# NSA gates projected inside the first query products, in two PSUM banks, with another order of weight splits around the compression

## The chip, the cores and the metric

The kernel runs on one core of one Trainium2 chip. The metric is the device time of one execution in microseconds (us), lower is better. The program is hand-scheduled: every engine has its own written-out list of instructions, and semaphores are the only order between them.

## The reference, cut to what matters

Two decoder layers on 256 tokens of width 1024. Layer 0 mixes tokens with native sparse attention (NSA), layer 1 with latent attention; each is followed by a SwiGLU block, with RMSNorms around all of them. The change touches only the first part of the NSA mixer:

```
q, kc, vc, ks, vs, kw, vw, g = split(h @ w_in)     # 1024 | 6 x 256 | 48 columns
q = rope(q); ks = rope(ks); kw = rope(kw)
gates = sigmoid(g)                                 # 16 heads x 3 branches
k_cmp = rope(gelu(blocks(kc) @ cmp_w1_k) @ cmp_w2_k)   # 15 blocks of 32 tokens, 4 groups
v_cmp = gelu(blocks(vc) @ cmp_w1_v) @ cmp_w2_v
o = gate0 * attend(q, compressed) + gate1 * attend(q, selected) + gate2 * attend(q, window)
```

## The kernel before, in words

**Precision by splitting.** Weights arrive in float32 in one of three `raw` buffers (2048 columns each, SP's queue, `load`). ScalarE (ACT) rounds them to `w_hi` (`split_hi`, line 267), VectorE (DVE) writes the rest `raw - w_hi` to `w_lo` (`split_lo`, line 275). TensorE (PE) makes each product of three matmuls (`product`, lines 283 to 285): lo by hi, hi by lo, hi by hi. A chunk is 128 rows of the weight; two token tiles (t = 0, 1) of 128 tokens stand against each.

**Tiles and their waits.** The weights are numbered in one list of tiles n. A load of tile n waits until tile n-3 has been split (`lo_ready`); `split_hi` of tile n waits for its load and until tile n-3 has been used by PE (`weights_used`); `take` on PE waits for `split_lo`. Before the change tiles 0 to 5 are the key and value columns (512 columns by 4 chunks each), 6 the gates (48 columns by 8 chunks), 7 and 8 the compression weight of the keys (W1K), 9 and 10 that of the values (W1V), 11 to 13 the first queries (Q0: 3, 3 and 2 chunks of 256 columns), 14 to 16 the second queries (`NSA_Q1`), and so on.

**What PE runs, in order.** Key and value columns (`first_block`, `kv_block(1)`), 16 transposes of the compressed keys' and values' inputs (L982), `kv_block(2)`, the gates (48 matmuls of 48 columns into bank 2), `compress(0)` (48 matmuls with 60 stationary columns and 256 moving ones), 16 transposes of the keys (L1009), `compress(1)`, a transpose of the hidden layer (L1020), the first queries in bank 6, a second one, the compressed keys (L1033), eight transposes of the queries (L957), half of the second queries, a transpose of the compressed keys (L1066), the first scores (L842), the other half of the second queries, and then the attention's turns.

**What DVE and ACT run beside it.** ACT: splits, the evictions of PSUM (`ksv_out`, the copies to `c2T`), sine and cosine (L1428, L1429), the exponentials of the gates (L1469), the rounding of the block sums (`blk_hi`), GELU (L1481, L1490), `q_out`, `queries_out`. DVE: splits, the rotary angles (L1829 to L1843), the block sums (L1860), the other copies to `c2T` (L1878, L1880), `blk_lo` (L1865), which `compress` waits for, `rope` (L570 to L575), one plus the exponential and its reciprocal (L1896, L1897), and `masked` for the scores (L1697, L1702). The attention's first turn begins on DVE with `split_lo` of tile `NSA_Q1 + 3`.

Of the kernel before, what the change touches and what calls it, by code (L numbers as in the profile page):

```python
# [25 lines left out]
P = 128  # L26
# [15 lines left out]
GATES = 3 * HEADS  # L42
NOPE, ROPE = 64, 32
# [26 lines left out]
NSA_GATES = NSA_KV + 6  # L70
NSA_W1K = NSA_GATES + 1
# [26 lines left out]
def trunk(nc, x, positions, inv_freq, gains, lat_gain, nsa_w_in, pe_k, pe_v, w1_k, w1_v, w2_k, w2_v, nsa_w_out,  # L98
          mla_w_in, w_q_up, w_kv_up, mla_w_out, w_gate_up, w_down, out):
    with ExitStack() as ctx:  # L100
# [491 lines left out]
        def _(sp):  # L592
# [23 lines left out]
            def block_cols(lo, n):  # L616
                return slice(lo, lo + n)
# [116 lines left out]
        def _(pe):  # L734
# [251 lines left out]
            project_rows(NSA_GATES, [bank[2][:, t * GATES:(t + 1) * GATES] for t in range(T)], [KC], GATES)  # L986
# [70 lines left out]

            pe.wait_ge(sem("nsa_roped"), 1)
# [205 lines left out]
        def _(act):  # L1264
# [187 lines left out]
            split_hi(act, 6, KC * GATES)  # L1452
# [644 lines left out]
```

## Time and profile before

| what | value |
|---|---|
| median of 3 runs | 769.05 us (767.82 to 769.4) |
| profiled execution, its own time | 769.73 us |
| its span in the trace | 768.0 us, 9977 instructions |
| PE busy | 709.0 us, 92% |
| DVE busy | 425.6 us, 55% |
| ACT busy | 387.5 us, 50% |
| weights and other traffic | 111.02 MB, mean 145 GB/s |

Busy shares are means over the whole span. A matmul's recorded duration contains its way through the pipeline, so the distance from one start to the next is what it costs in a row of matmuls. The granted clock (PEclk) has two levels here: 1.00 is 2.4 GHz and 0.50 is 1.2 GHz.

### The profile page before, as it was taken

Reading aid. Unit: us, or ns where it says so; the run is one execution under the profiler, and the core shown is the slowest. Engines: PE = TensorE matmul, PEld = TensorE weight load, DVE = VectorE, ACT = ScalarE, POOL = GpSimd, SP = SyncE. Lnnn points to the kernel's source line nnn. Section 1 sums busy time; section 2 is a strip of 40 time slices with the busy share of each in tenths; the row PEclk is TensorE's granted clock in tenths of the full one; section 3 lists DMA queues with packets and bytes.
Section 4 is the critical chain, followed back from the end, with each engine's and each line's share of the span. In section 5 each row is a group of like instructions: output and inputs, shape, how many; then the busy total and the mean of one; then the engine's idle time right before and its main releaser. Section 6 shows DMA issues by size and latency. Waiting matters only on the chain.

```text
span 768.0 us, 9977 instructions
## 1 busy us (share of the span) xinstructions
PE 709.0 (92%) x3601; PEld 592.0 (77%) x3601; DVE 425.6 (55%) x887; ACT 387.5 (50%) x726; POOL 15.9 (2%) x39
## 2 busy tenths in 40 slices
PE   3999999899989999999997898998998999999995
PEld 2789877777868888888875697887776888888883
DVE  4567456577765444555456464535675554444554
ACT  6455365676653344443353456667636433334442
POOL 7000000000000000000000000000000000000000
PEclk9997999999999999999998979999899999999998
DMA  9662323113347544456551323343333555544421
GB/s 316 222 204 71 110 55 122 45 56 110 111 139 241 195 164 164 166 193 214 204 206 35 90 87 92 108 147 110 111 109 111 186 211 206 206 174 164 164 110 55
DMA packets 55921, 111.02 MB, mean 145 GB/s; under 512 B 4224, under 2 KB 15536, under 8 KB 55888
## 3 DMA queue, kind: packets, MB, share of 16 engines
q1 hardware_dynamic: 54544, 106.24, 41.3%
q0 software_dynamic: 1344, 4.35, 1.6%
q8 instruction: 19, 0.31, 0.2%
q14 instruction: 14, 0.11, 0.0%
HBM read 109.54 MB, written 1.05 MB: 144 GB/s over the span
## 4 chain that ended last, share of the span: by engine, by line
PE 78%; ACT 9%; DVE 8%; issue 3%; DMA 2%; SPq 0%; DVEq 0%; ACTq 0%
PE bank L283 23%; PE bank L284 22%; PE bank L285 22%; DVE w_lo L275 3%; ACT w_hi L267 3%; PE bank L842 2%; PE bank L862 2%; ACT s_sb L1324 1%; PE bank L759 1%; DMA raw<-in_nsa_w_in 1%; PE bank L909 1%; PE bank L872 1%; DMA raw<-in_mla_w_in 1%; PE bank L957 1%; PE bank L495 1%
## 5 line engine op out<-in xcount | busy, mean ns | idle before, releaser
L275 DVE TENSOR_TENSOR w_lo<-raw,w_hi 128x2048 fp32r<-128x2048 f32 (+6 forms) x112 | 209.4, 1886 | 83.8 <-ACT w_hi L267 83.6
L283 PE MATMUL bank<-w_hi,act_lo 128*128 128x512 f32 (+3 forms) x528 | 208.4, 395 | 13.9 <-DVE w_lo L275 9.5
L285 PE MATMUL bank<-w_hi,act_hi 128*128 128x512 f32 (+3 forms) x528 | 199.0, 377 | 0.0
L284 PE MATMUL bank<-w_lo,act_hi 128*128 128x512 f32 (+3 forms) x528 | 198.8, 377 | 0.0
L267 ACT ACTIVATE w_hi<-raw 128x2048 fp32r<-128x2048 f32 (+6 forms) x112 | 175.2, 1585 | 12.1 <-PE bank L285 10.3
L283 PEld LDWEIGHTS bank<-w_hi,act_lo 128*128 128x128 f32 x528 | 103.5, 196 | 35.5 <-issue 8.6
L284 PEld LDWEIGHTS bank<-w_lo,act_hi 128*128 128x128 f32 x528 | 103.7, 196 | 18.0 <-issue 1.9
L285 PEld LDWEIGHTS bank<-w_hi,act_hi 128*128 128x128 f32 x528 | 103.2, 195 | 17.9
L1268 ACT ACTIVATE hidT_hi<-bank 128x512 fp32r<-128x512 f32 x20 | 12.0, 598 | 168.1 <-PE bank L759 168.1
L1664 DVE TENSOR_TENSOR hidT_lo<-bank,hidT_hi 128x512 fp32r<-128x512 f32 x20 | 13.8, 692 | 134.2 <-ACT hidT_hi L1268 134.2
L284 PE MATMUL bank<-w_lo,hidT_hi 128*128 128x512 f32 x160 | 63.0, 394 | 0.0
L283 PE MATMUL bank<-w_hi,hidT_lo 128*128 128x512 f32 x160 | 62.9, 393 | 0.0
L285 PE MATMUL bank<-w_hi,hidT_hi 128*128 128x512 f32 x160 | 62.2, 389 | 0.0
L862 PE MATMUL bank<-big,pT 128*128 128x64 f32 x288 | 41.9, 275 | 3.6 <-ACT pT L1268 3.5
L862 PEld LDWEIGHTS bank<-big,pT 128*128 128x128 f32 x288 | 38.4, 197 | 6.4 <-ACT pT L1268 6.1
L283 PE MATMUL bank<-w_hi,part_lo 128*128 128x384 f32 (+2 forms) x96 | 35.7, 372 | 5.9 <-issue 2.1
L1324 ACT ACTIVATE s_sb<-s_sb,nmax 128x128 f32<-128x128 f32 (+1 forms) x66 | 29.5, 449 | 22.7 <-DVE nmax L1702 22.7
L283 PEld LDWEIGHTS bank<-w_hi,hidT_lo 128*128 128x128 f32 x160 | 30.0, 188 | 6.8
L285 PEld LDWEIGHTS bank<-w_hi,hidT_hi 128*128 128x128 f32 x160 | 30.0, 188 | 6.7
L284 PEld LDWEIGHTS bank<-w_lo,hidT_hi 128*128 128x128 f32 x160 | 30.1, 188 | 5.9
L1268 ACT ACTIVATE pT<-bank 128x256 f32<-128x256 f32 (+2 forms) x64 | 25.5, 398 | 16.5 <-PE bank L909 16.5
L284 PE MATMUL bank<-w_lo,part_hi 128*128 128x384 f32 (+2 forms) x96 | 33.3, 347 | 0.0
(212 smaller groups left out, 904.1 us busy)
## 6 DMA issues: line engine op xcount, KB each, us to landing
raw<-in_w_gate_up SPq DMA_DIRECT2D x44, 1024.0 KB, 5.3
raw<-in_w_down SPq DMA_DIRECT2D x22, 1024.0 KB, 5.0
raw<-in_nsa_w_in SPq DMA_DIRECT2D x6, 1024.0 KB, 9.7
raw<-in_w_q_up SPq DMA_DIRECT2D x8, 576.0 KB, 4.3
raw<-in_nsa_w_out SPq DMA_DIRECT2D x4, 1024.0 KB, 5.0
raw<-in_mla_w_in SPq DMA_DIRECT2D x4, 1024.0 KB, 6.2
raw<-in_mla_w_out SPq DMA_DIRECT2D x4, 1024.0 KB, 5.4
gain<-in_gains POOLq DMA_DIRECT2D x7, 512.0 KB, 5.8
```

The costliest lines, as they stand in the source:

```text
L267: ins = act.activation(hi[:, cols], raw[s][:, cols], ACT.Copy)
L275: ins = dve.tensor_tensor(lo[:, cols], raw[s][:, cols], hi[:, cols].bitcast(F32), ALU.subtract)
L283: pe.matmul(dst, a_lo, b_hi, start=start, stop=False)
L284: pe.matmul(dst, a_hi, b_lo, start=False, stop=False)
L285: return pe.matmul(dst, a_hi, b_hi, start=False, stop=stop)
L495: last = pe.transpose(bank[2 * t + b][:, c * P:(c + 1) * P], src(t, k), ident[:])
L759: last = pe.transpose(bank[2][:, c * SEQ + t * P:c * SEQ + (t + 1) * P], hid[:, t, c * P:(c + 1) * P], ident[:])
L842: pe.matmul(dst, q, k, start=True, stop=True).then_inc(sem(f"{m}_scores"), 1)
L862: last = pe.matmul(bank[4 if t == 0 else 7][:, b * KVW + i * HD:b * KVW + (i + 1) * HD], p, v, start=kt == 0, stop=kt == t)
L1268: return act.activation(dst, src, ACT.Copy)
L1324: ins = act.activation(v, v, ACT.Exp, bias=nmax[:, unit % 3, b:b + 1], scale=SEL_SCALE if nsa else MLA_SCALE, accum_out=rsum[:, t, i, b + ...
L1664: dve.tensor_tensor(lo[:].rearrange("p c s -> p (c s)"), bank[2][:], hi[:].rearrange("p c s -> p (c s)").bitcast(F32), ALU.subtract) \
```

## The change

The 48 gate columns move in the host's copy of `nsa_w_in` from the end to a place right behind the first 256 query columns, so that the first queries' tiles are 304 columns wide (`Q0W`) and carry the gates with them. The gates' own tile, its load, its two splits and its 48 matmuls go, and every later tile has a number lower by one (and so another of the three buffers). The first queries and gates go to banks 0 and 1 (one for each token tile) in place of bank 6, chunk by chunk for both token tiles, and the compressed keys are computed between the first and the second tile of them. The gates are first scaled out of PSUM (`gates_out`), the exponential follows in place, and the add and the reciprocal stand on DVE behind the second queries' rotation. The splits of tiles 3 to 5 go ahead of the rotary angles on DVE; sine and cosine go behind the split of the first compression tile on ACT.

```diff
-NSA_GATES = NSA_KV + 6
-NSA_W1K = NSA_GATES + 1
+NSA_W1K = NSA_KV + 6
 # SP
-            load(NSA_GATES, rows(nsa_w_in, 0, KC, block_cols(D + 6 * KVW, GATES)))
-            load_q(NSA_Q0, block_cols(0, KVW))
+            load_q(NSA_Q0, block_cols(0, Q0W))
 # PE
             kv_block(2)
             pe.wait_ge(sem("ksv_out"), 2 * T)
-            project_rows(NSA_GATES, [bank[2][:, t * GATES:(t + 1) * GATES] for t in range(T)], [KC], GATES)
...
-            pe.wait_ge(sem("gates_exp"), T)
+            pe.wait_ge(sem("kT_out"), 1)
             turn_hidc(0)
-            project_rows(NSA_Q0, [bank[6][:, t * KVW:(t + 1) * KVW] for t in range(T)], [3, 3, 2], KVW)
-            pe.wait_ge(sem("kT_out"), 1)
-            turn_hidc(1)
-            pe.wait_ge(sem("hidcT_out"), 1)
-            pe.wait_ge(sem("w2_loaded"), 32)
+
             pe.wait_ge(sem("kT_out"), 4)
-            for c in range(2):
-                last = pe.matmul(bank[4][0:CROWS, 0:HD], hidcT[:, c, :], w2[:, 0, c, :], start=c == 0, stop=c == 1)
-            last.then_inc(sem("kcmp_done"), 1)
+            for k in range(3):
+                take(pe, NSA_Q0 + k)
+                project(pe, NSA_Q0 + k, [bank[0][:, 0:Q0W], bank[1][:, 0:Q0W]], (3, 3, 2)[k], Q0W, 3 * k)
+                if k == 0:
+                    pe.wait_ge(sem("hidcT_out"), 1)
+                    turn_hidc(1)
+                    pe.wait_ge(sem("w2_loaded"), 32)
+                    for c in range(2):
+                        last = pe.matmul(bank[4][0:CROWS, 0:HD], hidcT[:, c, :], w2[:, 0, c, :], start=c == 0, stop=c == 1)
+                    last.then_inc(sem("kcmp_done"), 1)
...
+            q_part(NSA_Q1, range(6))
+            pe.wait_ge(sem("kcmp_roped"), 1)
+            pe.transpose(bank[5][0:HD, 0:CROWS], kcs[0:CROWS, :], ident[0:CROWS, 0:CROWS]).then_inc(sem("kcmp_turned"), 1)
             pe.wait_ge(sem("nsa_roped"), 1)
...
-            pe.wait_ge(sem("nsa_q_out"), T)
-            q_part(NSA_Q1, range(KC))
...
+            q_part(NSA_Q1, range(6, KC))
             pe.wait_ge(sem("padded"), 6)
+            pe.wait_ge(sem("gates_out"), T)
             scores("nsa", 0)
 # ACT
-            split_hi(act, 7, SLOT)
+            split_hi(act, 6, SLOT)
+            act.wait_ge(sem("angles"), 2)
+            act.activation(sin[:].rearrange("p t k -> p (t k)"), ang[:, 0, :], ACT.Sin).then_inc(sem("tables"), 1)
+            act.activation(cos[:].rearrange("p t k -> p (t k)"), ang[:, 1, :], ACT.Sin).then_inc(sem("tables"), 1)
+
             act.wait_ge(sem("blk_sum"), 1)
             copy(blk_hi[:].rearrange("p c n -> p (c n)"), blkf).then_inc(sem("blk_hi"), 1)
+            split_hi(act, 7, SLOT)
             ksv_out(2)
...
+            q_out("nsa", 0, NSA_Q0 + 2)
+            act.wait_ge(sem("gate_scale"), T)
+            for t in range(T):
+                scaled(gates[:, t, :], bank[t][:, KVW:Q0W], stat(0, t, 2)).then_inc(sem("gates_out"), 1)
+            split_hi(act, NSA_Q1 + 2, 2 * KVW)
+            act.wait_ge(sem("gates_out"), T)
+            act.activation(gates, gates, ACT.Exp).then_inc(sem("gates_exp"), 1)
 # DVE
+            split_lo(dve, 3, SLOT)
+            split_lo(dve, 4, SLOT)
+            split_lo(dve, 5, SLOT)
             dve.wait_ge(sem("pos_loaded"), 32)
...
-            dve.wait_ge(sem("gates_exp"), T)
-            gf = gates.rearrange("p t n -> p (t n)")
-            chain.link(dve.tensor_scalar(gf, gf, 1.0, None, ALU.add))
-            chain.link(dve.reciprocal(gf, gf))
...
             rotate("nsa", 1)
+            dve.wait_ge(sem("gates_exp"), 1)
+            gf = gates.rearrange("p t n -> p (t n)")
+            chain.link(dve.tensor_scalar(gf, gf, 1.0, None, ALU.add))
+            chain.link(dve.reciprocal(gf, gf))
```

On ACT, from the two roundings of the activations (`act_hi`) to the block sums' rounding (`part_hi`), before:

```order
L504 ACTIVATE act_hi<-bank 128x4x128 x2
L1428 ACT_TABLE_LOAD
L1428 ACTIVATE sin<-ang 128x48
L1429 ACTIVATE cos<-ang 128x48
L267 ACTIVATE w_hi<-raw 128x2048
L1271 ACTIVATE u<-bank,stats 128x1024 x2
L267 ACTIVATE w_hi<-raw 128x2048 x2
L1271 ACTIVATE big<-bank,stats 128x256 x4
L267 ACTIVATE w_hi<-raw 128x384
```

and the same place of ACT after the change:

```order
L504 ACTIVATE act_hi<-bank 128x4x128 x2
L267 ACTIVATE w_hi<-raw 128x2048
L1274 ACTIVATE u<-bank,stats 128x1024 x2
L267 ACTIVATE w_hi<-raw 128x2048 x2
L1274 ACTIVATE big<-bank,stats 128x256 x4
L1271 ACTIVATE big<-bank 64x4x128
L1271 ACTIVATE big<-bank 64x4x127
L1271 ACTIVATE big<-bank 64x4x128 x2
L267 ACTIVATE w_hi<-raw 128x2048
L1462 ACT_TABLE_LOAD
L1462 ACTIVATE sin<-ang 128x48
L1463 ACTIVATE cos<-ang 128x48
```

Sine and cosine moved behind the first compression tile's split, and the gates' split (128x384) is gone.

On PE, from the last matmul of the first queries to the scores, before (the 24 matmuls of half the second queries stand between the two pieces; the first scores are the row with L842):

```order
L285 MATMUL bank<-w_hi,act_hi 128x256
L1020 MATMUL bank<-ident,big 128x60 x2
L1033 MATMUL bank<-big 60x64 x2
L957 MATMUL bank<-ident,qs 64x128 x8
...
L285 MATMUL bank<-w_hi,act_hi 128x256
L1066 MATMUL bank<-ident,big 64x60
L842 MATMUL bank<-big,qT 128x256 x2
```

and after, from the last of the 18 matmuls of the second queries that now stand ahead of the transposes:

```order
L285 MATMUL bank<-w_hi,act_hi 128x256
L1062 MATMUL bank<-ident,big 64x60
L956 MATMUL bank<-ident,qs 64x128 x8
L283 MATMUL bank<-w_hi,act_lo 128x256
L284 MATMUL bank<-w_lo,act_hi 128x256
L285 MATMUL bank<-w_hi,act_hi 128x256
L283 MATMUL bank<-w_hi,act_lo 128x256
L284 MATMUL bank<-w_lo,act_hi 128x256
L285 MATMUL bank<-w_hi,act_hi 128x256
L841 MATMUL bank<-big,qT 128x256 x2
```

The hidden layer's transpose and the compressed keys went up between the queries' products, and 18 of the second queries' 24 matmuls now stand ahead of the queries' transposes.

On DVE, from the second queries' rotation (names `big` and `rope_tmp`) to the first split of the attention's turns, before:

```order
L573 TENSOR_TENSOR rope_tmp<-big,sin 128x64
L574 TENSOR_TENSOR big<-rope_tmp 128x8x8
L575 TENSOR_TENSOR big<-rope_tmp 128x8x8
L275 TENSOR_TENSOR w_lo<-raw,w_hi 128x768 x2
L1695 MEMSET waited 128x1
```

and after:

```order
L574 TENSOR_TENSOR big<-rope_tmp 128x8x8
L575 TENSOR_TENSOR big<-rope_tmp 128x8x8
L1919 TENSOR_SCALAR big<-big 128x96
L1920 RECIPROCAL big<-big 128x96
L275 TENSOR_TENSOR w_lo<-raw,w_hi 128x768 x2
```

The gates' add and reciprocal came in ahead of that split.

## Rows read from the trace of the kernel before

**Rows 1.** The page: clock in 40 slices, and the chain that ended last.

```profile
PEclk9997999999999999999998979999899999999998
...
PE 78%; ACT 9%; DVE 8%; issue 3%; DMA 2%; SPq 0%; DVEq 0%; ACTq 0%
```

**Rows 2.** Windows: start:end, length, each engine's busy time (instructions), clock, DMA.

```profile
41.88:43.54 1.66, 1.66 (x17) 1.66 (x16) 0.33 (x1) 1.46 (x5) 0.00 (x0) 1.00 0.99 332
43.54:54.52 10.98, 10.98 (x51) 9.10 (x50) 5.70 (x6) 5.57 (x8) 0.00 (x0) 1.00 0.69 227
54.52:57.23 2.71, 2.71 (x27) 2.71 (x25) 2.63 (x4) 2.51 (x5) 0.00 (x0) 1.00 0.87 229
57.23:62.10 4.87, 4.87 (x25) 4.87 (x25) 4.07 (x8) 2.14 (x2) 0.00 (x0) 0.50 0.36 103
62.10:67.47 5.37, 5.37 (x26) 5.37 (x27) 4.76 (x6) 2.29 (x3) 0.00 (x0) 0.50 0.19 64
67.47:70.19 2.72, 2.72 (x25) 2.71 (x24) 0.67 (x2) 1.92 (x1) 0.00 (x0) 0.99 0.54 148
70.19:73.35 3.16, 1.91 (x18) 1.67 (x16) 3.13 (x3) 2.88 (x4) 0.00 (x0) 1.00 0.04 3
73.35:79.10 5.75, 5.75 (x48) 5.55 (x49) 3.13 (x4) 2.32 (x4) 0.00 (x0) 1.00 0.41 115
79.10:85.31 6.21, 6.21 (x51) 6.01 (x51) 0.69 (x1) 1.05 (x3) 0.00 (x0) 1.00 0.37 106
85.31:87.86 2.55, 0.69 (x7) 0.49 (x6) 1.40 (x7) 2.44 (x6) 0.00 (x0) 1.00 0.00 0
87.86:91.41 3.55, 3.55 (x17) 3.33 (x18) 2.79 (x10) 3.45 (x8) 0.00 (x0) 0.52 0.39 111
91.41:93.48 2.07, 2.07 (x18) 1.87 (x17) 0.65 (x1) 0.00 (x0) 0.00 (x0) 1.00 0.66 201
```

**Rows 3.** PE's timeline: start, duration, instruction, idle before it and its releaser.

```profile
36.26 0.50 PE L283 MATMUL bank<-w_hi,act_lo 128*128 128x512 f32 x1 [0.74 <-DVE w_lo L275]
...
73.35 0.30 PE L283 MATMUL bank<-w_hi,part_lo 128*60 128x256 f32 x1 [1.26 <-issue]
...
87.86 1.83 PE L957 MATMUL bank<-ident,qs 128*64 128x128 f32 x8 [1.86 <-DVE qs L575]
...
457.62 0.34 PE L284 MATMUL bank<-w_lo,part_hi 128*128 128x384 f32 x1
457.80 0.34 PE L285 MATMUL bank<-w_hi,part_hi 128*128 128x384 f32 x1
```

**Rows 4.** ACT's timeline, the same columns.

```profile
42.08 1.57 ACT L1271 ACTIVATE big<-bank,stats 128x256 f32<-128x256 f32 x4 [2.59 <-PE bank L285]
...
43.93 2.44 ACT L1268 ACTIVATE big<-bank 64x512 f32<-64x512 f32 x4
...
67.87 1.92 ACT L267 ACTIVATE w_hi<-raw 128x2048 fp32r<-128x2048 f32 x1 [3.27 <-PE bank L285]
```

**Rows 5.** DVE's timeline, the same columns.

```profile
51.29 2.29 DVE L275 TENSOR_TENSOR w_lo<-raw,w_hi 128x2048 fp32r<-128x2048 f32 x1 [2.91 <-ACT w_hi L267]
53.50 0.68 DVE L1878 COPY big<-bank 64x512 f32<-64x512 f32 x1
...
56.33 1.16 DVE L1865 TENSOR_TENSOR part_lo<-big,part_hi 128x960 fp32r<-128x960 f32 x1
...
60.33 0.28 DVE L570 TENSOR_TENSOR rope_tmp<-big,cos 128x128 f32<-128x128 f32 x1
...
62.16 1.90 DVE L1860 TENSOR_TENSOR big<-big 128x480 f32<-128x480 f32 x2
...
67.08 0.75 DVE L1897 RECIPROCAL big<-big 128x96 f32<-128x96 f32 x1
...
100.66 0.96 DVE L275 TENSOR_TENSOR w_lo<-raw,w_hi 128x768 fp32r<-128x768 f32 x1 [0.56 <-ACT w_hi L267]
```

**Rows 6.** DMA issues of the first 115 us: count, KB each, us to landing.

```profile
raw<-in_w_k SPq DMA_DIRECT2D x2, 1024.0 KB, 6.7
```

More of the change, by code:

```diff
@@ L42 @@
 GATES = 3 * HEADS
+Q0W = KVW + GATES
 NOPE, ROPE = 64, 32
@@ L622, in _ @@
                 for half in range(2):
-                    load(NSA_KV + 2 * b + half, rows(nsa_w_in, 4 * half, 4, block_cols(D + 512 * b, 512)))
+                    load(NSA_KV + 2 * b + half, rows(nsa_w_in, 4 * half, 4, block_cols(D + GATES + 512 * b, 512)))
                     if b == 0 and half == 0:
                         sp.dma_start(h[:, 1, :], x[P:2 * P, :]).then_inc(sem("x_loaded1"), 16)
-            load(NSA_GATES, rows(nsa_w_in, 0, KC, block_cols(D + 6 * KVW, GATES)))
             for first, w in ((NSA_W1K, w1_k), (NSA_W1V, w1_v)):
@@ L1019, in turn_hidc @@
                 for c in range(2):
-                    last = pe.transpose(bank[2 + v][:, c * 64:c * 64 + CROWS], hidc[0:CROWS, v, c * P:(c + 1) * P],
+                    at_ = v * P + c * 64
+                    last = pe.transpose(bank[3][:, at_:at_ + CROWS], hidc[0:CROWS, v, c * P:(c + 1) * P],
                                         ident[0:CROWS, 0:CROWS])
                 last.then_inc(sem("hidc_turned"), 1)
-            pe.wait_ge(sem("gates_exp"), T)
+            pe.wait_ge(sem("kT_out"), 1)
             turn_hidc(0)
-            project_rows(NSA_Q0, [bank[6][:, t * KVW:(t + 1) * KVW] for t in range(T)], [3, 3, 2], KVW)
-            pe.wait_ge(sem("kT_out"), 1)
-            turn_hidc(1)
-            pe.wait_ge(sem("hidcT_out"), 1)
-            pe.wait_ge(sem("w2_loaded"), 32)
-            pe.wait_ge(sem("kT_out"), 4)
-            for c in range(2):
-                last = pe.matmul(bank[4][0:CROWS, 0:HD], hidcT[:, c, :], w2[:, 0, c, :], start=c == 0, stop=c == 1)
-            last.then_inc(sem("kcmp_done"), 1)
+            pe.wait_ge(sem("kT_out"), 4)
+            for k in range(3):
[8 more added lines that the diff above has]
+                    last.then_inc(sem("kcmp_done"), 1)
             def block_values():
@@ L1382, in q_out @@
                     for t in range(T):
-                        scaled(qs_of["nsa"][to % 2][:, t, :], bank[6][:, t * KVW:(t + 1) * KVW], pre_scale(0, t)) \
+                        src = bank[t][:, 0:KVW] if to == 0 else bank[6][:, t * KVW:(t + 1) * KVW]
+                        scaled(qs_of["nsa"][to % 2][:, t, :], src, pre_scale(0, t)) \
                             .then_inc(sem("nsa_q_out"), 1)
@@ L1425, in _ @@
             turn_act(act, "u0", 1)
-            act.wait_ge(sem("angles"), 2)
-            act.activation(sin[:].rearrange("p t k -> p (t k)"), ang[:, 0, :], ACT.Sin).then_inc(sem("tables"), 1)
-            act.activation(cos[:].rearrange("p t k -> p (t k)"), ang[:, 1, :], ACT.Sin).then_inc(sem("tables"), 1)
             split_hi(act, 3, SLOT)
@@ L1843, in _ @@
             dve.tensor_scalar(a1, a2, -1.0, math.pi / 2, ALU.mult, ALU.add).then_inc(sem("angles"), 1)
-            split_lo(dve, 3, SLOT)
-            split_lo(dve, 4, SLOT)
-            split_lo(dve, 5, SLOT)
-            split_lo(dve, 6, KC * GATES)
             def block_sum(v):
@@ L1872, in _ @@
             block_sum(0)
-            split_lo(dve, 7, SLOT)
+            split_lo(dve, 6, SLOT)
             for t in range(T):
@@ L1882, in _ @@
             block_lo(0)
-            split_lo(dve, 8, SLOT)
+            split_lo(dve, 7, SLOT)
             dve.wait_ge(sem("ksv_out"), 4 * T)
@@ L1891, in _ @@
             block_sum(1)
+            split_lo(dve, 8, SLOT)
+            block_lo(1)
             split_lo(dve, 9, SLOT)
-            dve.wait_ge(sem("gates_exp"), T)
-            gf = gates.rearrange("p t n -> p (t n)")
-            chain.link(dve.tensor_scalar(gf, gf, 1.0, None, ALU.add))
-            chain.link(dve.reciprocal(gf, gf))
-            split_lo(dve, 10, SLOT)
-            block_lo(1)
             dve.wait_ge(sem("padded"), 6)
@@ L1905, in _ @@
                     .then_inc(sem("kT_out"), 1)
-            split_lo(dve, 11, 3 * KVW)
-            split_lo(dve, 12, 3 * KVW)
-            split_lo(dve, 13, 2 * KVW)
-            rotate("nsa", 0)
-            split_lo(dve, NSA_Q1, 3 * KVW)
-            split_lo(dve, NSA_Q1 + 1, 3 * KVW)
+            split_lo(dve, 10, 3 * Q0W)
+            split_lo(dve, 11, 3 * Q0W)
+            split_lo(dve, 12, 2 * Q0W)
             dve.wait_ge(sem("kcmp_done"), 1)
@@ L1915, in _ @@
             rope(chain, kcs[0:CROWS, :], 8, cos[0:CROWS, T, 0:16:2], sin[0:CROWS, T, 0:16:2], [8], sem("kcmp_roped"))
+            split_lo(dve, NSA_Q1, 3 * KVW)
+            split_lo(dve, NSA_Q1 + 1, 3 * KVW)
+            rotate("nsa", 0)
             split_lo(dve, NSA_Q1 + 2, 2 * KVW)
@@ L2064 @@
     layers = 2
+    w_in = np.asarray(nsa_w_in)[0]
     pos = np.asarray(positions)[0]
@@ L2077 @@
         "lat_gain": np.concatenate([np.asarray(mla_q_norm), np.asarray(mla_kv_norm)], axis=1),
-        "nsa_w_in": np.asarray(nsa_w_in)[0],
+        "nsa_w_in": np.concatenate([w_in[:, 0:KVW], w_in[:, D + 6 * KVW:], w_in[:, KVW:D + 6 * KVW]], axis=1),
         "pe_k": np.ascontiguousarray(np.asarray(nsa_cmp_pe_k)[0].reshape(CK, P).T),
```

24 lines of the change are left out of this document (6 added, 18 removed).

## The prediction

> **What bounds the kernel now.** I read the page first: the chain that ended last is 78% PE, ACT and DVE 9% and 8%, DMA 2% [rows 1]. So time goes only where PE gets less to do, waits less or has a faster clock. The clock row shows which stretch is poor: 9 in nearly every slice, but 7 in the fourth (57.6 to 76.8 us), exactly where the change works, and some 8s and a 7 later [rows 1]. The windows cut that stretch by what PE does [rows 2]. The reader is to see five things there.
>
> 1. `kv_block(2)` ends at 54.52, and the gates take from there to 62.10: 2.71 us at 1.00, then 4.87 us at 0.50. They are 48 matmuls of only 48 columns. Their first half costs 0.11 us each, about what a 60-by-256 compression matmul costs (5.75/48 = 0.12), so the gates cost time out of proportion to their columns.
> 2. The clock was 1.00 through the 512-column matmuls and fell at 57.23, 2.7 us after the narrow ones began. `compress(0)` therefore ran its first 25 matmuls at 0.50 (5.37 us, 0.215 each), and the other 23 at 0.99 (2.72 us, 0.118 each). (A window's count also has what only overlaps its edge.)
> 3. From 70.19 to 73.35 PE does the 16 key transposes and waits 1.26 us [rows 2, 3]. The wait ends with `blk_lo(1)` on DVE, which stands behind tile 10's split, whose ACT half sat 3.27 us waiting for PE to use tile 7 [rows 4].
> 4. After the first queries (to 85.31) PE waits 1.86 us for their rotation [rows 3], and the clock is low until 91.41: 3.55 us for eight transposes and nine or ten matmuls.
> 5. Before all this, PE waits 0.74 us at 36.26 for tile 3's `split_lo` [rows 3], which DVE runs only behind the rotary angles.
>
> **The change, part by part.** The sum is made against the profiled execution, 769.73 us with a span of 768.0; it is 0.7 above the median of the three runs, so I take the saving off the median, 769.05.
>
> *Splits 3 to 5 ahead of the angles.* The split needs neither the angles nor the tables, only tile 0 used, which is over 8 us earlier. It ends some 4 us ahead of the need, and the 0.74 us wait goes. With the first matmul's slower start: **-0.8**. Later tiles' loads start earlier with it.
>
> *The gates' tile goes.* 2.71 + 4.87 = 7.58 us of PE. Is something else late then? `compress(0)` needs `blk_lo(0)`, and its chain starts at the end of `kv_block(1)`, as PE's does. PE: 16 transposes 1.66 and `kv_block(2)` 10.98, together 12.6 us [rows 2]. ACT: before, evictions and copies ended at 46.37, 4.5 us after 41.88 [rows 4]; without the gates' ACT split (0.4) 4.1. DVE then: block sum 1.9, split 2.3, four copies 2.8, `blk_lo` 1.16 [rows 5], 8.2. Together 12.3 us: 0.3 less than PE. Angles (2.8 us on DVE) and sine and cosine now lie in time in which DVE and ACT wait (DVE sat 2.91 us ahead of 51.29 [rows 5]); without that cover they would cost 2.8 and 1.7. The gates' matmuls are gone in full; if DVE comes up to 1 us late, that much is lost.
>
> *Clock in the compression.* What stood ahead of the fall was 48-column work. Now 512-column matmuls run up to `compress(0)`, which at 1.00 raised and kept the clock itself (67.47 to 70.19). 48 at 0.118 are 5.65 in place of 8.09: **-2.4**. No row shows `compress(0)` straight behind `kv_block(2)`; the bounds are 0 (it falls anyway) and 2.4. I take 2.4, since `compress(1)` ran 5.75 us at 1.00 even behind transposes and a wait.
>
> *The second compression.* Its weight's tiles are numbers 8 and 9 and wait for tiles 5 and 6, used earlier than 6 and 7 were. So `blk_lo(1)` is bound by DVE alone: from `kv_block(2)`'s end `ksv_out(2)` 1.8, rotation 1.8, block sum 1.9, tile 8's split 2.3, `blk_lo` 1.16 [rows 4, 5]: 9.0 us. PE's way there is 5.65 + 1.75 = 7.4 us, so PE waits 1.6 us, not 1.3. From 54.52 to 73.35 were 18.83 us; 9.0 of them remain: **-9.8** for gates, clock and this wait together (7.6 + 2.4 - 0.2).
>
> *Loads.* W1V's second tile is issued after tile 6's split, at about 49; 6.7 us to landing [rows 6] make 56, and its ACT split can start only at 56.4, when `compress(0)` has used tile 6. The later ones (467 KB) have as much room. Cost nothing; 1 us late costs nothing either, since PE takes that tile at about 65.
>
> *First queries and gates in one.* From `compress(1)`'s end to the first scores were 6.21 + 2.55 + 3.55 + 2.07 = 14.4 us [rows 2]. Now: 0.25 for `hidc`; 48 matmuls of 304 columns; 0.55 for `hidc` and compressed keys; 18 matmuls of the second queries; 0.2; eight transposes; 6 matmuls; the scores. No row has 304 columns: 256 cost 0.120 from start to start, 384 cost 0.18 [rows 3], so on the line between them 0.14 (bounds 0.12 and 0.18, 5.8 to 8.6 us), 6.8 us. 24 matmuls of the second queries at 0.12 are 2.9 (18 of them 2.2, 6 of them 0.7). The transposes at full clock are 0.9 (16 took 1.66). The rotation (1.5 us on DVE) starts after the last matmul of the first queries, and its cover is the 18 matmuls, 2.2 us: with `q_out` 1.0 ahead it ends 2.5 after, so 0.2 of wait stays. Sum 0.25 + 6.8 + 0.55 + 2.2 + 0.2 + 0.2 + 0.9 + 0.7 = 11.8: **-2.5**. The queries' copies on ACT now have the exponential's table ahead of them (1.3 us), but it starts while DVE rotates, so 0.1 at most. The bank waits (`kT_out`) are over 2 us early.
>
> *Add and reciprocal in front of the attention.* 0.2 + 0.75 us on DVE [rows 5], behind the second rotation and ahead of the split that PE waits for. DVE was idle 0.56 us there, waiting for ACT [rows 5]: **+0.4**. Queued behind it: that split, and behind it the next scores' masks.
>
> Sum: -0.8 - 9.8 - 2.5 + 0.4 = -12.7. From there the instructions are the same, only with other buffer numbers, and no later wait is tied to absolute time: loads are released by splits. 769.05 - 12.7 = **756.4 us**.
>
> **The rivals.**
>
> *A. Another fall of the clock.* The key transposes and a now longer wait (3.3 us together) stand between the compressions. For it: at 85.31 to 87.86 transposes, small matmuls and a wait came before a stretch at 0.52. Against it: 3.16 us of the same kind at 70.19 were followed by 1.00 [rows 2]. Price as in `compress(0)`: 25 matmuls at 0.215 in place of 0.118, +2.4: 758.8. The Trainium skill ("TensorE: Matmul & The Clock Gate", Part 4: PE-mode transpose) says that transposes do not count as busy for the clock. By that rule the fall would come and the time would be 758.8; the row at 70.19 to 73.35 does not show it.
>
> *B. DVE late.* The margin of 0.3 us at `blk_lo(0)` is gone if the copies run beside splits slower than before. Up to +1: 757.4.
>
> *C. The saving is given back.* Falls of the clock in the latent mixer (slices with 8, 7, 8 [rows 1]) depend on when they come; and if the wider tiles or earlier weights hit each other, loads reappear as waits. A 7 means about a fifth of 19 us at half speed, some 2 us. Two more such: 761 to 764.
>
> *D. Slower.* The clock, once fallen between the compressions, stays at 0.50 through the first and second queries, since the change makes them short pieces with waits between. 48 compression matmuls cost +0.095 each (4.6), 48 of 304 columns at half speed about +0.12 (5.8), 24 of 256 columns +0.095 (2.3), then the second half of the second queries 2.3: 15 us, more than 12.7, so 771.4. It decides only if nearly all of these 144 matmuls are slow; against it, matmuls of 256 columns brought the clock back at 67.47 and at 91.41 [rows 2].
>
> *E. The change does not do what it says*: the fall at 57 us and the wait at 36 us stay, and DVE's chain eats the gates. That would need 7 us more on DVE than the rows have.
>
> **How the numbers follow.** 756.4 with its own spread of 754.5 to 757 has 0.60; B 0.12; A 0.17; C 0.07; D 0.02; E 0.02. Range: the likeliest, B and A, with about 1 us for the spread of the runs before and 1 us below for a wait that I price too high: 753.8 to 760.2 leaves C, D and E and a little of A out. A measurement can tell 0.2%, 1.5 us: faster needs 767.5 or less. Faster 0.96, same 0.02, slower 0.02.
>
> **What would show it.** First key matmul of `kv_block(1)`'s second half at about 35.4 without a wait; `compress(0)` at 53.5 to 53.8, at clock 1.00, 5.7 us long; `compress(1)` at 62.5 to 63 behind a wait of about 1.6 us; 304-column matmuls 0.14 us apart; first scores at 80 to 81; the attention's first split 0.4 us later against the scores. Wrong would make it: 0.50 anywhere between 54 and 80 us, `blk_lo(0)` after 54, or a difference between the two traces' first scores (13 us) that is not still there at the end.

## The result, and the profile after

The changed kernel takes 757.64 us (median of 4 runs, 755.48 to 764.27), the kernel before 769.22 us beside it (4 runs, 767.82 to 772.12): a ratio of 0.9849, with a 95% interval of 0.9806 to 0.9893. Run again on another chip it was 758.49 us (6 runs) beside 772.99 (11 runs), 0.9811 (0.9771 to 0.9850). The forecast was 756.4, with a range of 753.8 to 760.2. The profiled execution took 756.18 us, with a span of 754.5.

The page of the changed kernel, with the same two rows as [rows 1]: the clock in 40 slices of 18.9 us, and the shares of the chain that ended last.

```profile
PEclk9999999999999999999999989998999999999998
...
PE 75%; DVE 10%; ACT 9%; issue 3%; DMA 2%; SPq 0%; DVEq 0%; ACTq 0%
```

The 7 of the fourth slice is gone. The chain has a little less PE and a little more DVE: the waits that are left end with DVE. The windows of the changed kernel, cut at the same places as [rows 2] (start:end, length, busy time of each engine with its instructions, clock, DMA share, GB/s), show each stage:

```profile
42.25:53.23 10.98, 10.98 (x52) 9.04 (x50) 8.42 (x10) 8.64 (x11) 0.00 (x0) 1.00 0.48 153
53.23:58.85 5.62, 5.62 (x50) 5.61 (x48) 5.45 (x10) 5.18 (x6) 0.00 (x0) 1.00 0.40 120
58.85:62.17 3.32, 1.91 (x18) 1.67 (x16) 3.32 (x3) 3.04 (x4) 0.00 (x0) 1.00 0.05 6
62.17:67.93 5.76, 5.75 (x49) 5.56 (x49) 5.42 (x5) 2.41 (x4) 0.00 (x0) 1.00 0.51 135
67.93:71.52 3.59, 3.59 (x28) 3.22 (x27) 0.79 (x1) 1.39 (x4) 0.00 (x0) 1.00 0.85 223
71.52:75.79 4.27, 4.27 (x32) 4.27 (x31) 2.56 (x9) 1.96 (x4) 0.00 (x0) 1.00 0.33 73
75.79:78.03 2.24, 2.24 (x21) 2.11 (x19) 1.46 (x6) 2.02 (x6) 0.00 (x0) 1.00 0.66 178
78.03:80.06 2.03, 1.85 (x17) 1.72 (x16) 0.93 (x3) 2.02 (x6) 0.00 (x0) 1.00 0.49 161
80.06:83.83 3.77, 3.77 (x30) 3.67 (x29) 1.26 (x12) 0.45 (x3) 0.00 (x0) 1.00 0.28 70
83.83:88.65 4.82, 2.69 (x26) 1.85 (x25) 3.76 (x15) 4.43 (x18) 0.00 (x0) 1.00 0.00 0
```

From top to bottom: `kv_block(2)`, `compress(0)`, key transposes and wait, `compress(1)`, the first queries with the gates in two pieces, 18 matmuls of the second queries, the queries' transposes and the last six matmuls, and in the last two rows the first scores up to the attention's first split. The reader is to see the clock column: 1.00 in every row, where [rows 2] had 0.50 from 57.23 to 67.47 and 0.52 from 87.86 to 91.41. The second row stands where two rows of 5.37 and 2.72 us and the gates' two rows stood.

PE's timeline of the changed kernel shows what is left of the waits (start, duration, instruction, idle before it and its releaser), and how far apart the wide matmuls of queries and gates are:

```profile
62.17 0.30 PE L283 MATMUL bank<-w_hi,part_lo 128*60 128x256 f32 x1 [1.42 <-DVE part_lo L1866]
...
68.71 0.30 PE L283 MATMUL bank<-w_hi,act_lo 128*128 128x304 f32 x1
68.85 0.30 PE L284 MATMUL bank<-w_lo,act_hi 128*128 128x304 f32 x1
...
78.44 0.41 PE L956 MATMUL bank<-ident,qs 128*64 128x128 f32 x2 [0.18 <-DVE qs L575]
...
88.65 0.36 PE L283 MATMUL bank<-w_hi,act_lo 128*128 128x256 f32 x1 [0.93 <-DVE w_lo L275]
```

The wait at 36.26 in [rows 3] has no counterpart. Set side by side, the five parts of the stretch that the prediction summed are (before and after by [rows 2] and the windows above; the stretch before the attention is also read from the second execution of the changed kernel):

| stretch, us | before | after | after, again | difference | forecast |
|---|---|---|---|---|---|
| start to the end of `kv_block(2)` | 54.52 | 53.23 | 52.74 | -1.3 | -0.8 |
| from there to the start of `compress(1)` | 18.83 | 8.94 | 8.96 | -9.9 | -9.8 |
| `compress(1)` | 5.75 | 5.76 | 5.74 | 0.0 | 0 |
| its end to the first scores | 14.38 | 12.13 | 12.15 | -2.25 | -2.5 |
| first scores to the attention's first split | 8.29 | 8.59 | 8.59 | +0.3 | +0.4 |
| sum, at the split's first matmul | 101.77 | 88.65 | 88.18 | -13.1 | -12.7 |

The span of this execution fell by 768.0 - 754.5 = 13.5 us, so nearly all of it is there at the first split. In the second execution of the changed kernel it is not so: 13.6 us are saved at the first split, but its span of 757.1 us is only 10.9 below, and its clock row has 8, 8, 8 in three slices where the first execution has 9, 9, 8 (last section).

### The profile page after: what moved, and what is told of

Same layout as the page of the kernel before. It is cut to its first block, busy times and chain, and to the rows that moved or that the text cites. A ratio compares the mean times of both kernels' runs of the same rounds, so it can differ in the third digit from the quotient of the medians.

```text
span 754.5 us, 9892 instructions
## 1 busy us (share of the span) xinstructions
PE 697.0 (92%) x3553; PEld 580.4 (77%) x3553; DVE 424.9 (56%) x886; ACT 387.2 (51%) x724; POOL 15.9 (2%) x39
## 3 DMA queue, kind: packets, MB, share of 16 engines
q0 software_dynamic: 1344, 4.35, 1.6%
HBM read 109.54 MB, written 1.05 MB: 147 GB/s over the span
## 4 chain that ended last, share of the span: by engine, by line
PE 75%; DVE 10%; ACT 9%; issue 3%; DMA 2%; SPq 0%; DVEq 0%; ACTq 0%
PE bank L283 22%; PE bank L284 21%; PE bank L285 21%; DVE w_lo L275 4%; ACT w_hi L267 3%; PE bank L841 2%; PE bank L861 2%; ACT s_sb L1327 1%; DMA raw<-in_nsa_w_in 1%; PE bank L758 1%; PE bank L908 1%; PE bank L871 1%; PE bank L495 1%; DMA raw<-in_mla_w_in 1%; ACT s_sb L346 1%
## 5 line engine op out<-in xcount | busy, mean ns | idle before, releaser
L283 PE MATMUL bank<-w_hi,act_lo 128*128 128x512 f32 (+3 forms) x512 | 202.8, 396 | 13.4 <-DVE w_lo L275 9.0
L285 PE MATMUL bank<-w_hi,act_hi 128*128 128x512 f32 (+3 forms) x512 | 193.8, 378 | 0.0
L284 PE MATMUL bank<-w_lo,act_hi 128*128 128x512 f32 (+3 forms) x512 | 193.7, 378 | 0.0
L283 PEld LDWEIGHTS bank<-w_hi,act_lo 128*128 128x128 f32 x512 | 98.5, 192 | 34.8 <-issue 9.3
L284 PEld LDWEIGHTS bank<-w_lo,act_hi 128*128 128x128 f32 x512 | 98.6, 193 | 18.0 <-issue 1.9
L285 PEld LDWEIGHTS bank<-w_hi,act_hi 128*128 128x128 f32 x512 | 98.5, 192 | 18.0
```

Of the source, the lines that this page charges most:

```text
L283: pe.matmul(dst, a_lo, b_hi, start=start, stop=False)
L284: pe.matmul(dst, a_hi, b_lo, start=False, stop=False)
L285: return pe.matmul(dst, a_hi, b_hi, start=False, stop=stop)
```

## The experiments

**1. Gates' matmuls wide, in their old place.** The kernel before, but each of the 48 matmuls of the gates has 256 columns in place of 48. The added columns hold other numbers of the same weight buffer and nobody reads their products.

```diff
-            project_rows(NSA_GATES, [bank[2][:, t * GATES:(t + 1) * GATES] for t in range(T)], [KC], GATES)
+            take(pe, NSA_GATES)
...
+                    tok, cols = slice(t * P, (t + 1) * P), slice(c * GATES, c * GATES + WIDE)
+                    last = product(pe, bank[2][:, t * 256:t * 256 + WIDE], act_hi[:, c, tok], act_lo[:, c, tok],
+                                   g_hi[:, cols], g_lo[:, cols], c == 0, c == KC - 1)
```

> The kernel before, but each of the 48 gate matmuls has 256 moving columns in place of 48 (the further columns are leftovers in the weight buffer and are not read); nothing else changes. Theory: narrow matmuls let the clock fall, and wide ones would not. The 48 matmuls then take 48 x 0.12 = 5.8 us in place of 7.6, at clock 1.00, and the compression behind them 5.7 us in place of 8.1: 4.2 us less than before, about 765, although PE is given five times the columns. Rival, the clock falls by itself about there: both stages at 0.215 us a matmul for the most part, no gain, 769.

Measured: 770.39 us (10 runs, 767.43 to 775.68) beside 771.93 (13 runs), ratio 0.9985 (0.9951 to 1.0019). Windows of its trace, from the gates on:

```profile
53.66:59.36 5.70, 5.70 (x49) 5.70 (x48) 4.97 (x5) 4.67 (x6) 0.00 (x0) 1.00 0.59 188
59.36:64.98 5.62, 5.62 (x50) 5.62 (x49) 5.45 (x10) 4.23 (x4) 0.00 (x0) 1.00 0.25 71
64.98:67.47 2.49, 1.91 (x18) 1.64 (x15) 2.42 (x4) 2.21 (x4) 0.00 (x0) 1.00 0.30 62
67.47:69.85 2.38, 0.00 (x1) 0.03 (x1) 2.35 (x3) 2.15 (x3) 0.00 (x0) 0.87 0.32 105
69.85:76.83 6.98, 6.98 (x49) 6.80 (x49) 3.03 (x4) 0.84 (x1) 0.00 (x0) 0.80 0.35 94
```

Five times the columns and yet faster: gates 5.70 and `compress(0)` 5.62, together 11.32 us where [rows 2] has 15.67. So it was the narrow matmuls, not the amount of work, that the low clock followed. But the 4.35 us come back out further on: PE now waits 2.96 us in place of 1.26 for DVE's chain (+1.7), and behind that wait the clock falls after all, so that `compress(1)` takes 6.98 in place of 5.75 us (+1.2). Of the 4.35 us 1.4 are left, less than the total can tell from nothing. This is also the place where the fall of rival A is seen, in one trace. The low clock has about 2.8 us of `compress(1)` (estimated from its mean of 0.80), some 13 matmuls at 0.215 us.

**2. That wait filled.** The same kernel with 12 dead matmuls of 512 columns behind the key transposes.

```diff
                     last.then_inc(sem("k_turned"), 1)
+            for c in range(12):
+                pe.matmul(bank[6][:], act_hi[:, c % KC, 0:P], act_hi[:, c % 4:c % 4 + 2, :], start=True, stop=True)
             pe.wait_ge(sem("c2T_k"), 2)
```

> The kernel before with its gates' matmuls 256 columns wide (where the clock stayed at its high level through the gates and the first compression, but fell between the two compressions, behind 16 transposes and a wait of 2.96 us), and now 12 dead matmuls of 512 columns between those transposes and the wait; they go into a bank that nobody reads. Theory: what let the clock fall there is the stretch in which PE did only transposes or nothing, so with the wait filled (12 x 0.23 = 2.7 us) the second compression runs at 1.00 and takes 5.75 us in place of 6.98. Rival: the fall comes from something else (a moment in time, the narrow output of the compression), and the second compression still has slow matmuls at its start.

Measured: one run, 768.8 us. Windows of its trace, the key transposes, the filler and `compress(1)`:

```profile
65.04:66.70 1.66, 1.66 (x18) 1.66 (x16) 1.59 (x4) 1.40 (x3) 0.00 (x0) 1.00 0.10 10
66.70:69.89 3.19, 3.02 (x16) 2.19 (x13) 3.16 (x3) 2.96 (x5) 0.00 (x0) 1.00 0.45 122
69.89:75.63 5.74, 5.74 (x49) 5.54 (x49) 3.03 (x4) 0.84 (x1) 0.00 (x0) 1.00 0.42 115
75.63:89.72 14.09, 11.31 (x90) 10.37 (x89) 5.54 (x17) 6.96 (x16) 0.00 (x0) 1.00 0.35 102
```

and of PE's timeline in the last of these windows:

```profile
84.39 1.06 PE L958 MATMUL bank<-ident,qs 128*64 128x128 f32 x8 [1.86 <-DVE qs L576]
...
88.65 0.38 PE L284 MATMUL bank<-w_hi,act_lo 128*128 128x256 f32 x1 [0.93 <-DVE w_lo L276]
```

`compress(1)` is back at 5.74 us at 1.00, as expected with the stretch filled. It is one execution, and falls vary between executions (below), so it supports the cause without proving it. Its last window adds a surprise: here PE waited 1.86 us for the rotation of the first queries just as in [rows 3], and no fall followed. Yet this stretch, up to the first scores, took 14.09 us and not much less than the 14.38 of the kernel before with its fall: at full clock PE ran ahead and then waited 0.93 us for DVE's split of the second queries' last tile (88.65). So in the old order the low clock of [rows 2] was worth only 0.3 us there; what it cost the matmuls, a wait would have cost for the most part.

**3. Narrow matmuls put back into the changed kernel**, dead ones, between `kv_block(2)` and `compress(0)`. No tile, no exponential and no wait comes with them.

```diff
             pe.wait_ge(sem("ksv_out"), 2 * T)
+            for t in range(T):
+                for c in range(KC):
+                    tok = slice(t * P, (t + 1) * P)
+                    product(pe, bank[2][:, t * GATES:(t + 1) * GATES], act_hi[:, c, tok], act_lo[:, c, tok],
+                            act_hi[:, c, 0:GATES], act_lo[:, c, 0:GATES], c == 0, c == KC - 1)
```

> The changed kernel with 48 dead matmuls of 48 columns put back between the sixth tile's matmuls and the first compression (they multiply the activations by a slice of the activations, into a bank that nobody reads; no weight tile, no exponential, no wait of their own). They cost PE the same time as the removed gates. If narrow matmuls in that place let the clock fall, they take 7.6 us (half of them at 0.11, half at 0.215), and the first compression runs its first half at the low clock, 8.1 in place of 5.6 us; the wait before the second compression (1.42 in the changed kernel) goes down to nothing, since DVE has more time. From the end of kv_block(2) to the start of the second compression then 7.6 + 8.1 + 2 = 17.7 in place of 8.9 us, and the total 8 to 9 us above the changed kernel, 765 to 767 beside 757.6. Rival: the fall in the kernel before came from its waits for the gates' tile or from a moment in time; then the dead matmuls cost 48 x 0.11 = 5.3, the first compression stays at 5.6, and with the wait taken up the total is 4 us above, about 761.5.

Measured: 766.89 us (10 runs, 765.11 to 770.71) beside 771.28 (17 runs), ratio 0.9936 (0.9902 to 0.9970). Windows of its trace, `kv_block(2)`, the narrow matmuls at either clock, `compress(0)`, transposes and wait, `compress(1)`, and the stretch to the first scores:

```profile
42.35:53.33 10.98, 10.98 (x52) 9.10 (x50) 8.42 (x10) 8.63 (x11) 0.00 (x0) 1.00 0.48 159
53.33:57.40 4.07, 4.07 (x38) 4.07 (x37) 3.90 (x8) 3.37 (x5) 0.00 (x0) 0.99 0.36 95
57.40:59.77 2.37, 2.37 (x13) 2.37 (x13) 2.37 (x3) 0.00 (x0) 0.00 (x0) 0.50 0.29 100
59.77:67.40 7.63, 7.63 (x49) 7.63 (x50) 1.23 (x1) 1.92 (x1) 0.00 (x0) 0.71 0.22 61
67.40:69.96 2.56, 1.91 (x18) 1.67 (x16) 1.26 (x2) 2.28 (x4) 0.00 (x0) 1.00 0.01 3
69.96:75.72 5.76, 5.76 (x49) 5.56 (x49) 5.42 (x5) 3.17 (x4) 0.00 (x0) 1.00 0.22 59
75.72:87.85 12.13, 11.95 (x91) 11.31 (x90) 5.75 (x17) 7.39 (x18) 0.00 (x0) 1.00 0.55 150
```

The fall returns with them: the clock is 1.00 up to there, and `compress(0)` takes 7.63 us instead of 5.62. From the end of `kv_block(2)` to `compress(1)` are 16.63 us in place of 8.94, so the narrow matmuls cost 7.7 us here, 6.44 by themselves and 2.0 through the clock of `compress(0)`, less 0.8 of wait. The two ratios to the kernel before (0.9936 here, 0.9849 and 0.9811 for the changed kernel) put it at 7 to 10 us of the total. I expected 8.8. The fall came 4.07 us after their start and not 2.71, which makes it 1.6 less, and of the wait 0.65 us stayed, where I had expected nothing. The rival (4 us, no fall) is out. `compress(1)` and the stretch to the first scores are as in the changed kernel, at 1.00.

So the fall came in both traces with narrow matmuls in this place (the kernel before and this one) and in none of the eight without them. What it is about them that brings the fall is not shown.

**4. The queries' section in its old order.** The changed kernel, but the first queries' rotation is covered by nothing again, and all second queries come behind the transposes. The hidden layer's transpose, the compressed keys and the rows of ACT and DVE that belong to them also go back to the old order.

```diff
-            q_part(NSA_Q1, range(6))
-            pe.wait_ge(sem("kcmp_roped"), 1)
-            pe.transpose(bank[5][0:HD, 0:CROWS], kcs[0:CROWS, :], ident[0:CROWS, 0:CROWS]).then_inc(sem("kcmp_turned"), 1)
             pe.wait_ge(sem("nsa_roped"), 1)
...
-            q_part(NSA_Q1, range(6, KC))
+            q_part(NSA_Q1, range(KC))
```

> The changed kernel (gates in the 304 columns, banks 0 and 1), but with the query section in the order of the kernel before: all first queries, then the hidden layer's transpose and the compressed keys, then the queries' transposes, then the second queries; DVE and ACT rows as before too. Theory: PE waits some 1.9 us for the rotation again (0.2 in the changed kernel) and with the transposes that lets the clock fall once more: 1.7 us, and 1.4 us more if the clock falls: 2 to 3.3 us slower than the changed kernel, about 759 to 760.5. Rival, this order is worth nothing and all the gain is the gates': no difference.

Measured: 761.82 us (4 runs, 759.54 to 767.61), ratio 0.9882 (0.9815 to 0.9949). Windows of its trace: first queries with gates, the wait, and the transposes with the second queries.

```profile
68.25:75.39 7.14, 7.14 (x51) 6.90 (x51) 0.79 (x1) 1.13 (x3) 0.00 (x0) 1.00 0.53 148
75.39:77.95 2.56, 0.70 (x8) 0.50 (x7) 1.35 (x6) 2.45 (x8) 0.00 (x0) 1.00 0.00 0
77.95:83.75 5.80, 5.80 (x33) 5.26 (x34) 3.60 (x10) 3.91 (x9) 0.00 (x0) 0.71 0.48 136
```

Wait and fall are both back, and the stretch is 15.50 us in place of 12.13: +3.4. The wide matmuls alone make the stretch *longer* than before (15.50 against 14.38, since the gates' columns ride in it), so the saving there is all the order's: cover of the wait and clock together, which this run does not separate (experiment 2 puts the clock's share in the old order at 0.3 us). The total went up by 2.5 us or more by the ratios (0.9882 here, 0.9849 and 0.9811 for the changed kernel), but the intervals overlap, so the stage is what shows it.

**5. Angles, sine and cosine in their old place** in the changed kernel, on DVE ahead of the splits 3 to 5, and on ACT where they were.

```diff
+            act.wait_ge(sem("angles"), 2)
+            act.activation(sin[:].rearrange("p t k -> p (t k)"), ang[:, 0, :], ACT.Sin).then_inc(sem("tables"), 1)
+            act.activation(cos[:].rearrange("p t k -> p (t k)"), ang[:, 1, :], ACT.Sin).then_inc(sem("tables"), 1)
...
-            split_lo(dve, 3, SLOT)
-            split_lo(dve, 4, SLOT)
-            split_lo(dve, 5, SLOT)
             dve.wait_ge(sem("pos_loaded"), 32)
```

> The changed kernel, but the rotary angles on DVE stand ahead of the splits of tiles 3 to 5 again, and sine and cosine on ACT ahead of tile 3's split. Theory: PE waits 0.74 us for tile 3 again and everything behind is later by that: 0.8 to 0.9 us slower than the changed kernel. Rival, the early angles relieve ACT and DVE ahead of the compressions and give it back: no difference.

Measured: 758.01 us (4 runs, 757.59 to 762.33), ratio 0.9842 (0.9791 to 0.9893): not to be told from the changed kernel. Its trace has the wait again:

```profile
36.90 0.50 PE L283 MATMUL bank<-w_hi,act_lo 128*128 128x512 f32 x1 [0.76 <-DVE w_lo L275]
```

All later stages have the lengths of the changed kernel within 0.01 us (8.95, 12.13 and 8.58 us in the table's second, fourth and fifth rows), so the order of splits works in the first row alone. `kv_block(2)` ended at 52.74 to 53.55 in six traces without this wait, and at 53.66 to 55.15 in four with it. Most of the spread inside each group has another source, and it can be taken out. PE's first products (from 15.0 to 15.4 us on) stand 0.43 us apart at first and 0.23 later, and the change comes at another moment in each execution: after 10 matmuls in the kernel before, after 7 or 8 in the changed one, after 14 here. Four transposes come behind them, in the kernel before and in the changed one at

```profile
21.51 0.60 PE L495 MATMUL bank<-ident,u 128*128 128x128 f32 x4
```

```profile
21.29 0.60 PE L495 MATMUL bank<-ident,u 128*128 128x128 f32 x4
```

(in this run at 22.18). From there to the end of `kv_block(2)` are 32.94 to 33.01 us in the four traces with the wait and 31.91 to 31.94 in the six without. So the order of splits is worth 1.05 us, and the rest of the -1.3 in the table is the start.

**6. Add and reciprocal behind the split.** The changed kernel with these two instructions of DVE moved.

```diff
             rotate("nsa", 1)
-            dve.wait_ge(sem("gates_exp"), 1)
-            gf = gates.rearrange("p t n -> p (t n)")
-            chain.link(dve.tensor_scalar(gf, gf, 1.0, None, ALU.add))
-            chain.link(dve.reciprocal(gf, gf))
...
                     split_lo(dve, NSA_Q1 + 3 + (n + 1) // 2, (3, None, 3, 2)[n] * KVW)
+                if n == 0:
+                    dve.wait_ge(sem("gates_exp"), 1)
+                    gf = gates.rearrange("p t n -> p (t n)")
+                    chain.link(dve.tensor_scalar(gf, gf, 1.0, None, ALU.add))
+                    chain.link(dve.reciprocal(gf, gf))
```

> The changed kernel with the add and reciprocal of the gates on DVE behind the first split of the attention's first turn in place of ahead of it. My theory: they hold up that split, and PE waits 0.93 us for it, 0.4 us more than in the kernel before; without them the wait is about 0.5 us and the total 0.4 us lower (757.2 beside 757.6, less than the totals can tell; the wait is what to read). Rival: the split waits for ACT's half in any case, and PE's wait stays at 0.93.

Measured: 762.05 us (6 runs, 755.52 to 763.95), ratio 0.9831 (0.9772 to 0.9890). DVE's timeline of the changed kernel, and then PE's and DVE's of this one:

```profile
86.52 0.20 DVE L1919 TENSOR_SCALAR big<-big 128x96 f32<-128x96 f32 x1
86.76 0.75 DVE L1920 RECIPROCAL big<-big 128x96 f32<-128x96 f32 x1
87.55 0.96 DVE L275 TENSOR_TENSOR w_lo<-raw,w_hi 128x768 fp32r<-128x768 f32 x1
```

```profile
88.49 0.36 PE L283 MATMUL bank<-w_hi,act_lo 128*128 128x256 f32 x1 [0.55 <-DVE w_lo L275]
```

```profile
87.39 0.96 DVE L275 TENSOR_TENSOR w_lo<-raw,w_hi 128x768 fp32r<-128x768 f32 x1 [0.56 <-ACT w_hi L267]
88.26 0.20 DVE L1936 TENSOR_SCALAR big<-big 128x96 f32<-128x96 f32 x1
```

The split no longer stands behind the reciprocal, and waits 0.56 us for ACT as in [rows 5]; PE waits 0.55 and not 0.93 us. From the first scores (80.28) to the split's matmul (88.49) are 8.21 us in place of 8.59: the 0.4 us of the forecast. The total can't show so little. It even reads 4 us more, and the clock says why: of the six runs two have a mean clock of 0.979 and take 755.52 and 755.69 us, four have 0.963 to 0.967 and take 760.84 to 763.95 (see the last section).

**7. Copies to ACT.** On top of 6, ACT takes half of the copies for the values' compression, and the second block sum comes ahead of the keys' rotation.

```diff
             split_hi(act, 7, SLOT)
+            act.wait_ge(sem("c_turned"), T + 2)
+            src = bank[1][:].rearrange("p (g s) -> p g s", g=4)
+            copy(c2T[1][0:HD, :, P:2 * P], src[0:HD]).then_inc(sem("c2T_v_half"), 1)
+            copy(c2T[1][HD:P, :, P - 1:2 * P - 1], src[HD:P, :, :]).then_inc(sem("c2T_v"), 1)
             ksv_out(2)
...
             split_lo(dve, 7, SLOT)
+            dve.wait_ge(sem("blk_lo"), 1)
+            dve.wait_ge(sem("c2T_v"), T)
+            dve.wait_ge(sem("c2T_v_half"), 1)
+            block_sum(1)
```

> On top of the late reciprocal, the second half of the copies for the values' compression goes from DVE to ACT, behind ACT's half of the split of tile 7, and the second block sum comes ahead of the keys' rotation on DVE (behind a wait for the end of the first block's low half, which is long done). My theory: the 1.42 us wait of PE before the second compression ends with DVE's chain (rotation, block sum, split, blk_lo), so work taken out of it ends the wait about 0.8 us earlier, and the total is 1.2 us below the changed kernel on the same chip. Rivals: the copies on ACT delay its evictions of the selected keys and with them the rotation, so the wait stays or grows; or the first compression now waits for something.

Measured: 758.65 us (6 runs, 754.58 to 762.65), ratio 0.9825 (0.9780 to 0.9870), beside 758.49 for the changed kernel on the same chip. PE's, ACT's and DVE's timelines:

```profile
61.52 0.30 PE L283 MATMUL bank<-w_hi,part_lo 128*60 128x256 f32 x1 [0.65 <-issue]
```

```profile
59.23 1.01 ACT L1271 ACTIVATE part_hi<-big 128x960 fp32r<-128x960 f32 x1 [0.51 <-PE bank L285]
```

```profile
60.27 1.16 DVE L1870 TENSOR_TENSOR part_lo<-big,part_hi 128x960 fp32r<-128x960 f32 x1 [0.65 <-ACT part_hi L1271]
```

PE's wait before `compress(1)` is 0.65 us in place of 1.42, so the theory of that wait holds. What ends it now is ACT's half of the same block, which waits for PE's last matmul of `compress(0)` (the first block's halves lie in the same place), and DVE's half behind it. More than this the order can't give; a second buffer could, which was not tried. With the edit of 6 in it, the attention's first split comes at 87.61, 34.26 us after the end of `kv_block(2)`, against 35.42 in the changed kernel: 1.2 us less by the stages, and not visible in the totals.

**8. The changed kernel once more**, on the chip of 7.

> The changed kernel once more, beside the two others on one chip. By the runs so far 757.6 us (755.5 to 764.3), 1.5% below the kernel before; and in its profile the same lengths of the stages up to the attention's first split as in the first execution, within 0.1 us, wherever the clock falls later.

Measured: 758.49 us (6 runs, 755.87 to 761.61), and the stages of the table above, equal within 0.02 us from the end of `kv_block(2)` on. The first stage is not within the 0.1 us expected but 0.49 shorter, nearly all of it ahead of the transposes at 21.29 us (20.82 here).

## Why the prediction was right, step by step

- *The wait at 36 us.* Right: gone, and back at 0.76 us where the old order is restored (experiment 5). It was worth 1.05 us; 0.8 was forecast. Together with the earlier start this puts `compress(0)` at 53.23 and `compress(1)` at 62.17, ahead of the times forecast (53.5 to 53.8, 62.5 to 63).
- *The gates' own time and the clock of `compress(0)`.* Right, and the share of each is shown: narrow matmuls alone bring back 7.7 us in the changed kernel (experiment 3), and widening them in the kernel before lifts `compress(0)` to 1.00 (experiment 1). `compress(0)` took 5.62 us where 5.65 was forecast.
- *The wait before `compress(1)`.* Forecast 1.6 us, measured 1.42, and its cause, DVE's chain, is confirmed by experiment 7. The stretch of 9.0 us was 8.94.
- *Rival A*, a fall between the two compressions, did not come in any of five traces with 3.3 us of transposes and waiting in this place ([rows 2] had 3.16 us and none either). It is no empty fear, though: with 4.87 us there the fall came (experiment 1), and with the wait filled it did not (experiment 2), one trace each. It cost 1.2 us there and not the 2.4 that I had priced: the clock fell already in the wait (0.87), and some 13 matmuls were slow, not 25. The Trainium skill says ("TensorE: Matmul & The Clock Gate", Part 4: PE-mode transpose) that transposes do not count as busy. The prediction took from this that the fall would come; the rows at 58.85 and 62.17 do not show it, and they do not show either whether the transposes counted, since a stretch of 3.3 us without counted work need not bring a fall.
- *Rival B*, DVE late for `compress(0)`: the margin forecast was 0.3 us. In the changed kernel DVE's `blk_lo(0)` began at 51.70 and took 1.16 us; it ended at 52.86 and PE came at 53.23, 0.4 later. No wait.
- *Queries and gates in one.* 12.13 us, forecast 11.8. The 304-column matmuls are 0.14 us apart, as interpolated; the missing 0.3 us lie almost all in the first queries with `hidc` and compressed keys, 7.86 us where 7.6 were forecast. The remaining wait was put at 0.2 and is 0.18. What I had not seen is that the order carries more than the whole gain: experiment 4 gives back 3.4 us without it. Nor had I seen that the low clock from 87.86 to 91.41 hid another wait for DVE (experiment 2).
- *Add and reciprocal.* +0.4 forecast; the wait grew by 0.38 (0.55 to 0.93), the stretch by 0.30, and experiment 6 takes it off again.
- *Rival C*, the saving given back later: in the first execution 13.1 us were saved at the first split and 13.5 at the end, in the second 13.6 and 10.9. So 2.7 us were given back there, with a lower clock (mean 0.974 against 0.979) and equal stages up to the split; falls that come by execution explain it, a lasting cause is not shown. The price of this rival was misread: a 7 in the clock row is a mean of 0.7 to 0.8 in a slice, which is about half of its 19 us at half speed, not a fifth (in the fourth slice of [rows 1] from 57.6 to 67.47), and it cost there nearly 5 us, not 2. At that price two more would have made about 766. Rival D would have needed a clock at 0.50 across the queries; it was 1.00. E is out by the traces.

So the -12.7 of the sum stands against -13.1 in the traces, and against -11.6 and -14.5 in the medians on two chips. The mechanism was forecast part by part; that the sum came so near is also luck, since 0.5 us too little for the start stood against 0.25 too much for the queries, and that the median of four runs between 755.48 and 764.27 fell 1.2 us from the forecast is luck as well.

## What to carry to other kernels

Cost a matmul of few columns by its start-to-start time from the trace, not by its columns: 48 columns took 0.11 us where 256 took 0.12, so a small projection is cheap as added columns of a wider one (48 matmuls at 0.14 in place of 0.12 us, 1 us here), and dear as a tile of its own (7.6 us). Look at the clock of what comes *behind* narrow work and behind waits, and cover a wait with matmuls that have to be done anyway. A low clock in front of a wait may cost next to nothing (experiment 2), so follow the path to the next wait before pricing it. When a stage gets shorter, work out the next engine's chain before counting the gain (experiment 1 gave two thirds of its gain back).

## What the runs showed of the hardware

- Behind 48-column matmuls the clock fell from its upper to its lower level (1.00 to 0.50 of 2.4 GHz) with PE busy without a gap: 2.71 us after they began in the kernel before and 4.07 in experiment 3. With 256 columns in the same place it did not.
- The same stretch does not always fall. After the 1.86 us wait for the rotation the clock fell in the kernel before and in experiments 1 and 4, and stayed at 1.00 in experiment 2, which has the same instructions from `compress(1)` on as the kernel before.
- The spread of the totals goes with it. Page of the changed kernel in its second execution, and of experiment 6, which differs by two moved instructions:

```profile
PEclk9999999999999999999999888999899999999998
```

```profile
PEclk9999998999999999999998878999899999999998
```

and two windows of experiment 6, of which the changed kernel's first execution had both at 1.00:

```profile
100.00:120.00 20.00, 18.26 (x107) 15.92 (x107) 11.12 (x53) 11.89 (x40) 0.00 (x0) 0.83 0.29 99
160.00:180.00 20.00, 19.61 (x123) 16.22 (x122) 15.40 (x63) 13.94 (x44) 0.00 (x0) 0.91 0.34 106
```

With a mean clock of 0.979 the changed kernel took 755.5 to 756.5 us, with 0.974 758.4 to 759.1, with 0.963 764.3. Which stretches fall in an execution is worth up to 9 us, more than any single edit here save the gates' tile, and it hides edits of 1 us from the totals. What decides it is open.
